# A two-block transformer on one core: row fetches, modulation pieces, filler matmuls and closings moved around one projection

## The reference

```python
sh1x, s1x, g1x, sh2x, s2x, g2x = jnp.split(silu(c) @ ada_w[l] + ada_b[l], 6)   # and for c_ctx
ux = x * (1.0 + s2x) + sh2x
y = hier_moe(concat(ux, uc), ...)          # top 2 of 32 experts for each token
x = layer_norm(DEEPNORM_ALPHA * x + g2x * y, ln2_g[l], ln2_b[l])
# layer 1: ux = x * (1.0 + s1x) + sh1x, the same for ctx, then
q, k, v = split(z @ w_qkv)                 # c_w_qkv, 1024 x 3072, for x and for ctx
...
x = second_block(x, c_2, ctx_2, c_ctx_2, ada_w_2, ada_b_2, ...)   # needs silu(c_2) @ ada_w_2 + ada_b_2
```

## Time and profile before

| | us |
|---|---|
| median of 3 runs | 2502.62 (2501.89 to 2509.98) |
| the profiled execution | 2507.85 |
| its span | 2506.0 |
| TensorE busy in the span | 2253.3 |
| VectorE busy | 935.9 |
| stage of the projection, TensorE's first to last matmul | 942.12 to 1119.21 |
| TensorE idle in it ahead of a turn (L2160), longest | 5.47 |
| TensorE idle in it ahead of a closing (L490) | 5.88 and 2.00 |

### The profile page before, as it was taken

One profiled execution on the slowest core, in us unless ns is written; L12 is line 12 of the kernel. 1 busy time (PEld: TensorE's weight loads), 2 busy tenths in 40 slices (PEclk: granted clock), 3 DMA queues, 4 the chain that ended last, 5 costly groups with the idle time before them and its releaser, 6 DMA issues. The chain is left out here.

```text
span 2506.0 us, 35106 instructions
## 1 busy us (share of the span) xinstructions
PE 2253.3 (90%) x14014; PEld 1217.5 (49%) x14016; DVE 935.9 (37%) x1642; ACT 369.0 (15%) x631; POOL 135.1 (5%) x202
## 2 busy tenths in 40 slices
PE   5999877998888878986799999998999999989999
PEld 2443744543333324344433333333566777767776
DVE  3865667420000017778643111112433233582001
ACT  1000413111111111015211111110160000110000
POOL 1001010000000011010100000001201011000000
PEclk8999988999999998999899999999999999999999
DMA  9768421999999993790399999998315786524442
GB/s 359 281 246 329 162 70 68 369 423 423 423 423 422 422 408 115 267 363 30 137 385 421 423 421 422 423 421 313 128 52 206 267 306 239 166 97 154 155 155 74
DMA packets 174200, 687.10 MB, mean 274 GB/s; under 512 B 13813, under 2 KB 72181, under 8 KB 111648
## 3 DMA queue, kind: packets, MB, share of 16 engines
q1 hardware_dynamic: 159712, 625.38, 63.8%
q0 software_dynamic: 11392, 48.90, 5.4%
q10 hardware_dynamic: 3008, 11.62, 1.3%
HBM read 670.99 MB, written 13.81 MB: 273 GB/s over the span
## 5 line engine op out<-in xcount | busy, mean ns | idle before, releaser
L1647 PE MATMUL bank<-ring,arena 128*32 128x512 f32 (+1 forms) x3072 | 343.0, 600 | 27.8 <-DMA ring<-moe_w_up 15.1
L518 PE MATMUL bank<-ring,actT 128*128 128x512 f32 x768 | 337.0, 600 | 8.8 <-DMA ring<-ab_w_in 4.0
L2973 PE MATMUL bank<-actT,ring 128*128 128x256 f32 x1344 | 293.3, 379 | 0.0
L2973 PEld LDWEIGHTS bank<-actT,ring 128*128 128x128 f32 x1344 | 255.2, 190 | 42.3 <-issue 8.6
L1680 PE MATMUL bank<-arena 128*32 128x512 f32 (+1 forms) x2048 | 228.1, 597 | 21.2 <-ACT arena L1788 21.2
L518 PEld LDWEIGHTS bank<-ring,actT 128*128 128x128 f32 x768 | 146.7, 192 | 198.3 <-issue 194.2
L1856 DVE TENSOR_TENSOR arena<-arena,bank 128x512 f32<-128x512 f32 x32 | 22.0, 687 | 584.5 <-ACT arena L1783 584.5
L1647 PEld LDWEIGHTS bank<-ring,arena 128*32 128x32 f32 x3072 | 101.8, 111 | 263.2 <-issue 262.2
L596 DVE SCALAR_TENSOR_TENSOR arena<-ring,cols,arena 128x2048 f32<-128x2048 f32 x84 | 195.0, 2349 | 57.1 <-DMA ring<-ada_w 55.4
L2985 PE MATMUL bank<-ring,arena 128*128 128x512 f32 x352 | 154.6, 593 | 0.0
L2330 PEld LDWEIGHTS bank<-arena 128*128 128x128 bf16 x2304 | 133.0, 100 | 44.5 <-issue 36.1
(11 more groups left out here) (508 smaller groups left out, 2134.6 us busy)
## 6 DMA issues: line engine op xcount, KB each, us to landing
ring<-moe_w_gate SPq DMA_DIRECT2D x128, 1024.0 KB, 21.1
arena<-moe_w_down SPq DMA_DIRECT2D x128, 1024.0 KB, 21.3
ring<-ada_w SPq DMA_DIRECT2D x72, 1024.0 KB, 8.0
ring<-ffn_w SPq DMA_DIRECT2D x66, 1024.0 KB, 5.2
ring<-moe_w_up SPq DMA_DIRECT2D x64, 1024.0 KB, 23.4
actT<-moe_w_up SPq DMA_DIRECT2D x64, 1024.0 KB, 24.6
arena<-ada_w POOLq DMA_DIRECT2D x24, 1024.0 KB, 9.2
ring<-ab_w_in SPq DMA_DIRECT2D x14, 1024.0 KB, 8.3
```

What stands on the lines that cost most here:

```text
L518: mm = nc.tensor.matmul(self.bank[g % 6][:, :], lhsT(m, k), halves[k // 4][:, k % 4, :], start=(k == 0), stop=(k == KT - 1))
L1647: mm = nc.tensor.matmul(bank[j // 2][Q * q:Q * q + Q, :], A(XS + P * kt + Q * q, Q), weights(j, own, q, k * DE, DE), start=(kt == 0), stop ...
L2973: mm = nc.tensor.matmul(bank[2 - 2 * (j % 2) + which][:, f * SEQ:(f + 1) * SEQ], w[:, k, f * P:(f + 1) * P], self.actT[:, k * T:k * T + SE ...
```

## The change

Four things are moved.

1. GpSimd's fetches of tiles 0 and 1 wait for the last pair's piece 7 (`spare_in[0][1]`); those of tiles 2 and 3 still wait for piece 11.
2. Filler products of the identity with a constant tile, whose result nobody reads (`keep_warm`): two at the end of the experts of layer 0, six between the last rows' tiles 1 and 2.
3. The first three pieces of sum 0 are loaded by GpSimd into the arena instead of by SyncE into the ring, each once the tile of rows that lies there is turned. VectorE weighs them first; ScalarE waits at groups 6 and 12 until they are used, since its results go over them. The sums' later pieces are dealt out from group 3 on (`C_LATE` 3), so their last ones fall to groups 8, 13 and 17.
4. A closing comes two groups after its last piece instead of one (`lag=2`): behind groups 10, 15 and 19; the addition of the bias a group later, at most at group 19. GpSimd no longer waits for the last store at the end of this stage; SyncE does in the stage of the next experts, ahead of its load of that result. The other projection with sums, of layer 0, keeps its values.

```diff
-C_FIRST, C_LATE = 3, 4
+C_FIRST, C_LATE = 3, 3
+C_ASIDE = ((4096, 2), (6144, 4), (8192, 6))
+ASIDE_SPENT = {6: 1, 12: 3}
...
-        work = [3 if n in on_pe else 5 if lr in BOTH else 3 for n, lr in enumerate(rounds) for _ in range(KT)]
+        work = [3 if n in on_pe else 5 if lr in BOTH else 3 for n, lr in enumerate(rounds) for _ in range(KT)][aside:]
...
         def finished(g):
-            return [n for n in on_dve if g == min(last_group[n] + 1, len(groups) - 1)]
+            return [n for n in on_dve if g == min(last_group[n] + lag, len(groups) - 1)]
...
                 if front is not None:
                     front["power"](pool)
+                for k, (off, turned_at) in enumerate(aside):
+                    pool.wait_ge(sm["z_turned"].sem, sm["z_turned"].at(turned_at))
+                    self.unit_loads[k] += 1
+                    pool.dma_start(self.A(off, 2048), self.ada_piece(*rounds[0], k)).then_inc(self.unit_in[k], 16)
...
-                pool.wait_ge(ada_stored.sem, ada_stored.total)
+                if front is None:
+                    pool.wait_ge(ada_stored.sem, ada_stored.total)
...
+                    if aside and g in ASIDE_SPENT:
+                        act.wait_ge(ada_summed.sem, ada_summed.at(ASIDE_SPENT[g]))
                     act.wait_ge(self.pe_done.sem, self.pe_done.at(g + 1))
...
                 def weigh(n, l, r, k):
-                    self.arrived(dve, held[n, k])
-                    w = self.slot_view(held[n, k])
+                    if KT * n + k < len(aside):
+                        dve.wait_ge(self.unit_in[k], 16)
+                        w = self.A(aside[k][0], 2048)
+                    else:
+                        self.arrived(dve, held[n, k])
+                        w = self.slot_view(held[n, k])
...
-                        if g == min(last_group[n] + 2, len(groups) - 1):
+                        if g == min(last_group[n] + lag + 1, len(groups) - 1):
                             take(n)
...
                 else:
+                    sp.wait_ge(self.sem["ada_stored"].sem, self.sem["ada_stored"].total)
                     self.load_mod(sp, 2, 0, 2, (0,))
...
                 pair(more, LAST, own_last, lambda m: main_arrived(LAST, m), last=True)
+                if layer == 0:
+                    self.keep_warm(2)
...
-                    pool.wait_ge(self.spare_in[0][3], 16 * PAIRS)
-                    self.fetch(pool, nt, IDX, 0)
+                    pool.wait_ge(self.spare_in[0][1], 16 * PAIRS)
+                    for t in range(2):
+                        self.fetch(pool, nt, IDX, t)
                     pool.wait_ge(self.spare_in[0][5], 16 * PAIRS)
-                    for t in range(1, nt):
+                    for t in range(2, nt):
                         self.fetch(pool, nt, IDX, t)
...
+    def keep_warm(self, times):
+
+        for _ in range(times):
+            self.nc.tensor.matmul(self.bank[6][:, :], self.ident, self.misc[:, 0:512], start=True, stop=True)
...
             for t in range(4):
+                if t == 2:
+                    self.keep_warm(6)
                 self.combine(t, True, SG, 2 * t).then_inc(*up("last_mixed"))
```

More of the change, by code:

```diff
@@ L249, in __init__ @@
         self.unit_in = [ctx.enter_context(nc.semaphore(f"unit_in{n}")) for n in range(4)]
+        self.unit_loads = [0] * 4
     def signals(self, *names):
@@ L393, in spread, with hosted @@
         return [(g + 1) * n // groups - g * n // groups for g in range(groups)]
-    def hosted(self, rounds, groups, on_pe, late):
-        work = [3 if n in on_pe else 5 if lr in BOTH else 3 for n, lr in enumerate(rounds) for _ in range(KT)]
+    def hosted(self, rounds, groups, on_pe, late, aside=0):
+        work = [3 if n in on_pe else 5 if lr in BOTH else 3 for n, lr in enumerate(rounds) for _ in range(KT)][aside:]
         share, given = [], 0
@@ L406, in hosted, with plan_hosting @@
         return share
-    def plan_hosting(self, w, starts, order, rounds, on_pe=(), lead=0, first=1, late=0):
-        share = self.hosted(rounds, len(order), on_pe, late)
-        units = [(l, r, k) for l, r in rounds for k in range(KT)]
+    def plan_hosting(self, w, starts, order, rounds, on_pe=(), lead=0, first=1, late=0, aside=0):
+        share = self.hosted(rounds, len(order), on_pe, late, aside)
+        units = [(l, r, k) for l, r in rounds for k in range(KT)][aside:]
         asked = self.asked(order, lead, first)
@@ L425, in plan_ada, with ada_piece, st_linear_hosting @@
     def plan_ada(self, l, r, k):
-        w = (self.I["ada_w"], self.I["ada_w_2"])[l // 2][l % 2]
-        self.plan(w[k * P:(k + 1) * P, 2048 * r:2048 * (r + 1)].rearrange("(k p) n -> p k n", p=P), 1, 2048)
-    def st_linear_hosting(self, lhsT, groups, dest, rounds, sums, homes, pick, on_pe=(), lead=0, first=1, late=0, unmix=None, tables=None, beside=None, turned=None, front=None):
+        self.plan(self.ada_piece(l, r, k).rearrange("(k p) n -> p k n", p=P), 1, 2048)
+    def ada_piece(self, l, r, k):
+        return (self.I["ada_w"], self.I["ada_w_2"])[l // 2][l % 2][k * P:(k + 1) * P, 2048 * r:2048 * (r + 1)]
+    def st_linear_hosting(self, lhsT, groups, dest, rounds, sums, homes, pick, on_pe=(), lead=0, first=1, late=0, lag=1, aside=(), unmix=None, tables=None, beside=None, turned=None, front=None):
         nc, sm = self.nc, self.sem
-        share = self.hosted(rounds, len(groups), on_pe, late)
+        share = self.hosted(rounds, len(groups), on_pe, late, len(aside))
         last_of = {ci: g for g, (ci, m) in enumerate(groups)}
@@ L438, in st_linear_hosting @@
         after, at = [], 0
-        for n in share:
+        for g, n in enumerate(share):
+            n += len(aside) * (g == 0)
             after.append(units[at:at + n])
@@ L465, in ada @@
                         pe.wait_ge(ada_added.sem, ada_added.at(n - 1))
+                    if KT * n + k < len(aside):
+                        return
                     if n not in on_pe:
@@ L2543, in raise_sums @@
             nc.scalar.activation(A(LAM, 16), A(LAM, 16), ACT.Exp).then_inc(lam_exp.up(), 1)
-        self.st_linear_hosting(lambda m, k: self.actT[:, k * T + m * P:k * T + m * P + P], C_ORDER, dest, C_ROUNDS, C_SUMS, C_HOMES, C_PICK, C_ON_PE, lead=2, first=C_FIRST, late=C_LATE, unmix=A(XX, 2048), front=self.rows_before_c(),
+        self.st_linear_hosting(lambda m, k: self.actT[:, k * T + m * P:k * T + m * P + P], C_ORDER, dest, C_ROUNDS, C_SUMS, C_HOMES, C_PICK, C_ON_PE, lead=2, first=C_FIRST, late=C_LATE, lag=2, aside=C_ASIDE, unmix=A(XX, 2048), front=self.rows_before_c(),
                                beside=dict(pool=load_tables, dve=turn_angles, act=raise_sums))
@@ L3095, in weigh @@
                     layer = rounds[r][0]
-                    dve.wait_ge(self.unit_in[i % 4], 16 * (i // 4 + 1))
+                    dve.wait_ge(self.unit_in[i % 4], 16 * (i // 4 + 1 + self.unit_loads[i % 4]))
                     c = self.cols[:, 16 * (layer // 2) + k:16 * (layer // 2) + k + 1]
@@ L3342, in run @@
         self.plan_experts(0)
-        self.plan_hosting(I["c_w_qkv"][0], [512 * n for n in range(6)], C_ORDER, C_ROUNDS, C_ON_PE, lead=2, first=C_FIRST, late=C_LATE)
+        self.plan_hosting(I["c_w_qkv"][0], [512 * n for n in range(6)], C_ORDER, C_ROUNDS, C_ON_PE, lead=2, first=C_FIRST, late=C_LATE, aside=len(C_ASIDE))
         self.plan_linear(I["c_w_out"][0], 0, D)
```

1 line of the change is left out of this document (added).

## The result

The changed kernel took 2489.76 us (median of 6 runs, 2483.01 to 2496.06), the kernel before 2509.9 in the same comparison (6 runs, 2501.89 to 2514.33): a ratio of 0.9923 [0.99, 0.9946], 13.6 to 25 us less. The forecast was 2487.8, with a range of 2483 to 2496.5.

What follows compares the result with a forecast made beforehand. TensorE, busy for 90% of the span, was taken as the bound, with only its idle time and slow clock to win. 1.8 + 1.7 + 0.7 + 1.3 + 9.1 + 0.2 = 14.8 us off median 2502.62: 2487.8 us, range 2483 to 2496.5.

Steps and rivals of the forecast that it cites:

- part 1, fetches: End of layer 0's experts: earlier fetches remove VectorE's waits for tiles 0 and 1; 1.8 us, between 0.9 and 2.65.
- part 2, tile-0 sum: Start of the rows' sum: two fillers in the pause keep the clock full, 2.1 instead of 3.8 us; 1.7 us.
- part 2, turns and take: Turns and taking tile 1 ahead of the projection's groups: 2.0 instead of 2.7 us with the clock up; 0.7 us.
- part 2, groups 0 to 2: Projection's first groups: 23.36 us against 20.87 at full clock, 2.5 to be had, half of it taken; 1.3 us.
- part 3, pieces and closings: Projection's modulation sums: early pieces and later closings remove TensorE's waits of 5.9 and 2.0, clock 1.4, less 0.2; 9.1 us.
- part 4, the end: End of the projection's stage: next stage begins 2.8 to 3.1 us behind the last closing, before 3.24; 0.2 us.
- I take half: Groups 0 to 2: 1.3 of the possible 2.5 us, since TensorE's work behind the fillers is thin.
- The front gives nothing: Experts' end to first groups: fetch slows the last weights, clock falls twice; gain 10.8 us, time 2491.8; chance 0.18.
- The first closing still waits: First modulation sum: wait of 4 us or more, set by the ring's round trip; time 2493.0 or 2497; chance 0.11.
- GpSimd's pieces late: Modulation sums: pieces of GpSimd's queue come late, every later sum waits; slower, time 2507; chance 0.03.
- Within 5 us of before: Whole change without effect: fillers don't hold the clock, closings' waits reappear elsewhere; time 2499; chance 0.06.

Runs made afterwards that it cites:

- back alone: The changed kernel without the early fetch and the fillers (GpSimd's pieces, later closings and moved wait stay): 0.9931 [0.9915, 0.9946] of the kernel before.
- front alone: The kernel before with only the early fetch and the fillers added: 0.9978 [0.9962, 0.9993] of the kernel before.
- GpSimd waits: The changed kernel with GpSimd again waiting for the last store at the end of the projection's stage: one run, 2496.62 us.
- more fillers: The changed kernel with four fillers instead of two at the experts' end and four more between the last two pairs: 0.9918 [0.9904, 0.9932].

## Why the prediction was right, step by step

| step of the sum | forecast | measured, changed against before |
|---|---|---|
| part 1, fetches | 1.8 | 2.8; 2.0 as a mean over kernels |
| part 2, tile-0 sum | 1.7 | 0.8 |
| part 2, turns and take | 0.7 | 0.8 |
| part 2, groups 0 to 2 | 1.3 | 2.5 |
| part 3, pieces and closings | 9.1 | 9.8 |
| part 4, the end | 0.2 | 1.4 |
| sum | 14.8 | 18.2 |

**The number.** 2487.8 against 2489.76 is closer than the working deserves. The forecast started from 2502.62, the median of three runs; in six it was 2509.9. On that base the sum of 14.8 gives 2495.1, and the measured difference is 20.1 [13.6, 25]. So the gain was forecast some 5 us too small (inside the interval) from a base some 7 too low, and the closeness of the two times is luck.

**Part 1** held. Both waits went (in two other kernels with the early fetch 0.59 and 0.30 us of the first was left), and piece 11 was later by 2.4 us against before and 3.5 against the kernel that differs in the fetch alone, less than the 4 to 7 that was allowed for it and too little to delay the down product. The Trainium skill, page "DMA: Bandwidth & Descriptors", section "Queues, rings and completion order", which was weighed there, agrees with the trace as far as it goes: the fetch did not stand behind the down pieces, and these landed later for it.

**Part 2** is right in its sum (4.1 against 3.7) and not in its terms. The tile-0 sum was forecast at full clock, and this term failed, 0.8 us against 1.7: from 939.0 to 942.4 it ran at half, although the pause had shrunk from 6.97 to 2.14 us. Removing both end fillers left that stretch 3.4 us long (pause 4.06), and only the kernel with four there and four ahead of the pair was free of it: two at the end did nothing that the runs show. The groups gave all of their 2.5 us in this execution. "I take half" was a fair price: the clock stayed up in them in five of eight kernels with the six fillers, and in one of three without (back alone, 23.51 us). In none of those three was the stretch from 953 on at full clock throughout, but so few executions don't show that the fillers hold it.

**Part 3** held by its mechanism: pieces issued at 973.93 and 978.63 (forecast near 975 and 981), summed without a wait from 987.54, all closings free. The margin was thinner than forecast. TensorE was to come 1.6 us behind sum 0 and came 0.4 behind it; in two kernels it waited 0.53 and 0.42 us. Its two halves don't add. Against front alone, which has the same front and neither of them (last column 137.36), the lag without the pieces loses 4.1 us (141.43), the pieces without the lag gain 3.9 (133.50), and both gain 14.3 (123.04); against the kernel before (134.30) these are a loss of 7.1 and gains of 0.8 and 11.3. The moved wait is in all three. With GpSimd's wait kept, both together gain 6.7 (130.70 against 137.36). The working also counted VectorE's idle time for ring pieces at 13.7 us, the seven waits of L596; with L594's it was 27.6, and the 13.12 us at the first piece are what went. The Trainium skill, page "DMA: Bandwidth & Descriptors", section "Rules for kernel authors" (more queues bring no bandwidth), is not contradicted: the waits for the later ring pieces stayed at 13.2 us, and the gain came from pieces sent into a stretch in which the window of before shows 0.00 of the DMA in use.

**Part 4** is the step whose mechanism failed, 0.2 us against 1.4, on two counts. It had the next stage begin 2.8 to 3.1 us behind the last closing, after GpSimd's two issues; it began 1.80 behind it, at 1103.15, while the issues ran from 1102.49 to 1103.63 by the profile, whose spans on GpSimd are rough. And it held the moved wait to be nearly free either way, by the 3.24 us of before. The runs showed that the old place would have cost 7.2 us in the changed kernel. Without that edit the change would have been worth 10.4 us in this stretch (213.91 - 203.55), not 18.2.

**The rivals.** "The front gives nothing": with front alone the profile looks so (213.57 against 213.91), in the whole change it doesn't (the first four columns are 6.9 us shorter). "The first closing still waits": not in the change, but it is what the kernel with a lag of one does, 7.41 us. "GpSimd's pieces late": no wait for them in any kernel that has them. "Within 5 us of before": the difference is 13.6 us or more.

## What to carry to other kernels

Ask of a late wait whether its cause can start in a stretch where the DMA is idle, and of two edits to one wait whether they need each other: here later closings lost 4 to 7 us without the earlier pieces, the pieces gained 1 to 4 without the later closings, and both together gained 11 to 14. A stage that ends sooner meets other traffic: price the waits at its end anew, since a small store that landed after 2.8 us in the old order took 6.0 behind megabytes of loads here. And take the base of a forecast from as many runs as its terms deserve; three runs were off by half of the gain.

## What the runs showed of the hardware

- The same 8 KB store from GpSimd's queue at the end of this stage landed after 2.8 us (before, issued 0.8 us ahead of SyncE's loads) and 3.7 (front alone, 0.5 us ahead), and after 5.4 (changed) and 6.0 (GpSimd waits) where 4 MB of them had been issued ahead of it.
- Beside the early fetch (2 MB of rows) the last of the down pieces landed 3.5 us later behind the pair's start (20.85 against 17.36) than in the kernel with the late one.
- TensorE's clock: around the rows' sum a pause of 2.14 us went with 3.4 us at half clock (1.2 GHz), pauses of 4.06 and 4.74 with as much, those of 4.31, 5.81 and 6.97 with 6.6 to 6.9. With pauses of up to 2.02 us and busy matmuls ahead (the kernel with more fillers) it stayed at 2.4 GHz throughout. In the thin stretch of the turns it fell in three kernels and not in five with the same instructions there, so a profile of one execution says little about a clock term of 2 to 3 us.
